# The first expert block of a mixture-of-experts stage written ahead of its loop and of the block table, with 16-bit operands in the router

## What is computed

```python
logits = (h @ w_router).astype(jnp.float32) + b_router      # h: [512, 1024], 32 experts
topv, idx = lax.top_k(logits, TOP_K)                        # 4
gates = jax.nn.softmax(topv, axis=-1)
...
gu = xblk @ w_gate_up[e] + b_gate_up[e]                     # [1024, 2048] for each expert
gate = jnp.minimum(gu[:, :D_FF], SWIGLU_LIMIT)
up = jnp.clip(gu[:, D_FF:], -SWIGLU_LIMIT, SWIGLU_LIMIT)
act = (up + 1.0) * (gate * jax.nn.sigmoid(SWIGLU_ALPHA * gate))
return act @ w_down[e] + b_down[e]                          # [1024, 1024] for each expert
```

## Time and profile before

| | |
|---|---|
| median of 3 runs | 2981.27 us (2976.05 to 2981.37) |
| the profiled execution | 2982.14 us |
| its span in the trace | 2980.3 us |
| PE busy | 2805.3 us, 94% |
| DVE busy | 1319.7 us, 44% |
| ACT busy | 829.6 us, 28% |
| DMA in the span | 587.90 MB, mean 197 GB/s |
| weight chunks of the experts | 192 of 2048 KB, median 24.1 us from issue to landing |

### The profile page before, as it was taken

How to read it: one execution, slowest core, us unless ns; L and a number is a source line. 1 busy time by engine, 2 the same in 40 slices (tenths; PEclk the granted TensorE clock), 3 DMA queues, 4 the chain that set the end, 5 groups by cost and what they waited for, 6 DMA issues and landing times.

```text
span 2980.3 us, 44597 instructions
## 1 busy us (share of the span) xinstructions
PE 2805.3 (94%) x16220; PEld 1781.0 (60%) x16221; DVE 1319.7 (44%) x2773; ACT 829.6 (28%) x1663; POOL 103.1 (3%) x118
## 2 busy tenths in 40 slices
PE   9999999988999989998999899999999999999999
PEld 7888668743333333333333387585787695666884
DVE  6774686442232222222222455535564454444662
ACT  3321662212222222222222223414121224323211
POOL 0000000000000000000000000011000000110000
PEclk9999999978999999999999999999999999999999
DMA  3224312257999999999999831031321321112212
GB/s 143 85 71 138 120 52 85 76 209 317 416 423 415 414 410 410 414 413 407 412 413 413 337 117 69 29 110 36 106 85 57 105 101 43 68 64 78 85 57 85
DMA packets 115239, 587.90 MB, mean 197 GB/s; under 512 B 12714, under 2 KB 18218, under 8 KB 89507
## 3 DMA queue, kind: packets, MB, share of 16 engines
q1 hardware_dynamic: 105890, 569.26, 48.4%
q0 software_dynamic: 9216, 16.90, 1.5%
HBM read 572.91 MB, written 29.88 MB: 202 GB/s over the span
## 4 chain that ended last, share of the span: by engine, by line
PE 80%; DMA 12%; DVE 5%; issue 2%; ACT 2%; DVEq 1%; ACTq 0%; SPq 0%; POOLq 0%
PE banks L422 37%; DMA arena<-in_w_experts 11%; PE banks L1757 11%; PE banks L355 5%; PE banks L1799 5%; PE banks L989 4%; PE banks L916 3%; PE banks L1765 2%; PE banks L1805 2%; PE banks L1004 2%; PE banks L978 2%; PE banks L294 1%; PE banks L1243 1%; PE banks L952 1%; PE banks L1736 1%
## 5 line engine op out<-in xcount | busy, mean ns | idle before, releaser
L422 PE MATMUL banks<-arena 128*128 128x256 f32 (+2 forms) x5376 | 1156.1, 376 | 12.7 <-ACT arena L459 6.0
L422 PEld LDWEIGHTS banks<-arena 128*128 128x128 f32 x5376 | 1005.4, 190 | 147.8 <-issue 14.1
L1757 PE MATMUL banks<-arena 128*64 128x512 f32 x2048 | 466.7, 601 | 48.4 <-DMA arena<-in_w_experts 34.2
L1757 PEld LDWEIGHTS banks<-arena 128*64 128x64 f32 x2048 | 156.2, 137 | 315.2 <-issue 313.0
L459 ACT ACTIVATE arena<-banks 128x512 f32<-128x512 f32 (+2 forms) x220 | 129.9, 590 | 699.5 <-PE banks L422 696.6
L407 DVE TENSOR_TENSOR arena<-arena 128x1024 f32<-128x1024 f32 (+2 forms) x220 | 235.8, 1072 | 50.6 <-issue 26.4
L1938 DVE TENSOR_TENSOR arena<-banks,arena 128x512 f32<-128x512 f32 x64 | 44.3, 692 | 462.7 <-PE banks L1783 236.5
L1799 PE MATMUL banks<-arena 128*64 128x512 f32 x1024 | 237.8, 600 | 1.6 <-DMA arena<-in_w_experts 1.1
L475 DVE TENSOR_TENSOR arena<-banks,arena 128x512 f32<-128x512 f32 (+2 forms) x123 | 83.5, 680 | 273.6 <-PE banks L422 269.8
L355 PE MATMUL banks<-arena 128*128 128x512 f32 x384 | 166.8, 592 | 0.0
L1799 PEld LDWEIGHTS banks<-arena 128*64 128x64 f32 x1024 | 67.6, 135 | 129.1 <-issue 129.1
(11 more groups left out here) (269 smaller groups left out, 2388.3 us busy)
## 6 DMA issues: line engine op xcount, KB each, us to landing
arena<-in_w_experts SPq DMA_DIRECT2D x192, 2048.0 KB, 24.1
arena<-in_w_in SPq DMA_DIRECT2D x76, 1024.0 KB, 4.9
arena<-in_w_out SPq DMA_DIRECT2D x12, 1024.0 KB, 5.0
arena<-in_w_branch SPq DMA_DIRECT2D x24, 512.0 KB, 4.6
expert_rows<-arena SPq DMA_DIRECT2D x1, 8192.0 KB, 30.2
arena<-expert_rows SPq DMA_DIRECT2D x4, 2048.0 KB, 18.0
arena<-in_w_in SPq DMA_DIRECT2D x2, 2048.0 KB, 9.1
arena<-in_w_in SPq DMA_DIRECT2D x4, 832.0 KB, 4.9
```

What stands on the lines that cost most here:

```text
L422: last = PE.matmul(PS[:, bank, t * width:(t + 1) * width], one[:, t * P:(t + 1) * P], other, start=(first and t == 0 and kk == 0), stop=(t ...
L1757: last = PE.matmul(PS[HB * s:HB * (s + 1), 4 + h], xT[:, k, 0:HB], gate_up(2 * h + s, k), start=(k == 0), stop=(k == 7))
```

## The change

Router and experts are woven into each other. In the router, `oh`, the slot values (`slot_of`), the rows and the places they are compared with (`row_h`, `places_h`) become float16; the rows are scaled to whole numbers first. The gate matrix is built later, behind the keys. DVE's lists are made in two calls: the first block's alone, then (after `cnt`, `nb`, `cum`, block 0's `FEW` and `LAST`, and a new semaphore `first_rdy`) the other 191. PE, ACT and POOL start the expert stage at `first_rdy`. PE runs block 0 as code of its own, ahead of the loop, and between its products it does what the router's `pe_` did: ranking, keys, turning the gates, placing the table. SP still needs the table; it stores the gate matrix (`GATES_T`) and reads the last expert's row back in 96 copies, which takes the place of PE's product (line 1743). DVE makes the last block's selection in that block. The cut diff:

```diff
+        def rank_kinds(pe):
+            pe.wait_ge(SEM["kinds_rdy"], up(1))
+            PE.matmul(PS[:, 1, 200:202], v(CO["before"], P), v(KINDS, 2), start=True, stop=True)
+            PE.matmul(PS[:, 1, 202:204], v(CO["ones"], P), v(KINDS, 2), start=True, stop=True).then_inc(SEM["ranked"], 1)
+        def spread_keys(pe):
+            pe.wait_ge(SEM["keys_rdy"], up(1))
+            PE.matmul(PS[:, 1, 256:384], v(CO["ones"], P), v(KEYS, P), start=True, stop=True).then_inc(SEM["keys_mm"], 1)
+        def rows_of_table(pe):
+            pe.wait_ge(SEM["column_rdy"], up(1))
+            for q, col in enumerate((FOUND, FOUND + 4, FOUND + 5)):
+                last = PE.matmul(PS[0:1, 1, 64 * q:64 * q + 64], v(col, 1), v(PLACES, 64), start=True, stop=True)
+            last.then_inc(SEM["row_mm"], 1)
+        def turn_gates(pe):
+            pe.wait_ge(SEM["gmat_rdy"], up(1))
+            for tt in range(TT):
+                gates = v(R + 1536 + NE * tt, NE)
+                PE.transpose(PS[0:NE, 6, tt * P:(tt + 1) * P], gates, ident)
+                last = PE.matmul(PS[BS:P, 7, tt * P:(tt + 1) * P], gates, ident, start=True, stop=True, tile_position=(0, BS))
+            last.then_inc(SEM["gt_mm"], 1)
...
             lg, mx, ix, e4, idxf = (v2(R, TT, NE), v2(R + 128, TT, 8), v2(R + 160, TT, 8),
                                     v2(R + 192, TT, 4), v2(R + 208, TT, 4))
-            oh = v2(R + 256, 16, NE)
+            oh = v(R + 256, 8 * NE).bitcast(F16).rearrange("p (a e) -> p a e", a=16)
+            slot_of = v(R + 1856, 8 * LPE).bitcast(F16).rearrange("p (b a) -> p b a", b=LPE)
+            row_h, places_h = v(R + 768, 8).bitcast(F16), v(R + 784, P // 2).bitcast(F16)
...
             def dve_(dve, c):
...
                 V.memset(v(NOM, NE), 0.0)
-                oh4 = v3(R + 256, TT, 4, NE)
+                V.memset(v(BE, 1, 1), 0.0)
+                V.memset(v(BCOL, 1, 1), 0.0)
+                oh4 = oh.rearrange("p (t k) e -> p t k e", t=TT)
+                V.tensor_scalar(places_h, v(CO["iota_p"], P), 1.0 / PART, None, ALU.mult)
...
                     V.tensor_tensor(lg[:, tt], PS[:, tt, 0:NE], brow, ALU.add)
...
-                V.tensor_tensor(tmp, oh, v(GATES, 16).unsqueeze(2).to_broadcast([P, 16, NE]), ALU.mult)
-                V.drain()
-                V.tensor_reduce(Gm, v3(R + 896, TT, 4, NE).rearrange("p t k e -> p t e k"), AX.X, ALU.add)
-                V.drain().then_inc(SEM["gmat_rdy"], 1)
...
@@ -1556,14 +1568,16 @@
                 V.tensor_copy(blk_f, at_b)
                 V.drain()
                 V.scalar_tensor_tensor(row_f, blk_f, -float(BS * PART), addrf, ALU.mult, ALU.add)
+                V.drain()
+                V.tensor_scalar(row_h, row_f, 1.0 / PART, None, ALU.mult)
                 for b in range(LPE):
-                    V.scalar_tensor_tensor(v(R + 1856 + 16 * b, 16), blk_f, float(b), v(CO["slot1"], 16), ALU.is_equal, ALU.mult)
+                    V.scalar_tensor_tensor(slot_of[:, b], blk_f, float(b), v(CO["slot1"], 16), ALU.is_equal, ALU.mult)
                 V.drain()
                 for b in range(LPE):
-                    V.tensor_tensor(slots[:, :, b], oh, v(R + 1856 + 16 * b, 16).unsqueeze(2).to_broadcast([P, 16, NE]), ALU.mult)
+                    V.tensor_tensor(slots[:, :, b], oh, slot_of[:, b].unsqueeze(2).to_broadcast([P, 16, NE]), ALU.mult)
                 for tt in range(TT):
-                    V.tensor_tensor(rows_at[:, 4 * tt:4 * tt + 4], v(CO["iota_p"], P).unsqueeze(1).to_broadcast([P, 4, P]),
-                                    row_f[:, 4 * tt:4 * tt + 4].unsqueeze(2).to_broadcast([P, 4, P]), ALU.is_equal)
+                    V.tensor_tensor(rows_at[:, 4 * tt:4 * tt + 4], places_h.unsqueeze(1).to_broadcast([P, 4, P]),
+                                    row_h[:, 4 * tt:4 * tt + 4].unsqueeze(2).to_broadcast([P, 4, P]), ALU.is_equal)
                     V.drain().then_inc(SEM["addr_rdy"], 1)
...
+                def rows_of_lists(first, n):
+                    nobody, found_, rows_, tokens = (v(o + first, n) for o in (R + 1856, TAB + 1024, ALLR, ALLT))
+                    V.tensor_scalar(nobody, PS[:, 0, first:first + n], 0.0, float(1 << 20), ALU.is_equal, ALU.mult)
+                    V.drain()
+                    V.scalar_tensor_tensor(found_, PS[:, 0, first:first + n], -1.0, nobody, ALU.add, ALU.add)
+                    V.drain()
+                    V.tensor_copy(rows_.bitcast(I32), found_)
+                    V.drain()
+                    V.tensor_scalar(tokens.bitcast(I32), rows_.bitcast(I32), 2, None, ALU.logical_shift_right)
+                    V.drain()
+                dve.wait_ge(SEM["listed"], up(1))
+                rows_of_lists(0, 1)
+                V.tensor_copy(v(TOK, 1).bitcast(I32), v(ALLT, 1).bitcast(I32)).then_inc(SEM["tok_rdy"], 1)
                 V.tensor_copy(cnt, PS[:, 1, 128:160])
...
-                nobody = v(R + 256, LISTS)
-                dve.wait_ge(SEM["listed"], up(1))
-                V.tensor_scalar(nobody, PS[:, 0, 0:LISTS], 0.0, float(1 << 20), ALU.is_equal, ALU.mult)
-                V.drain()
-                V.scalar_tensor_tensor(v(R + 512, LISTS), PS[:, 0, 0:LISTS], -1.0, nobody, ALU.add, ALU.add)
-                V.drain()
-                V.tensor_copy(v(ALLR, LISTS).bitcast(I32), v(R + 512, LISTS))
-                V.drain()
-                V.tensor_scalar(v(ALLT, LISTS).bitcast(I32), v(ALLR, LISTS).bitcast(I32), 2, None, ALU.logical_shift_right)
-                V.drain()
-                V.tensor_copy(v(TOK, 1).bitcast(I32), v(ALLT, 1).bitcast(I32)).then_inc(SEM["tok_rdy"], 1)
+                V.tensor_scalar(v(FEW, 1, 1).bitcast(I32), cnt[0:1, 0:1], float(P // 2), None, ALU.is_le)
+                V.tensor_scalar(v(LAST, 1, 1).bitcast(I32), cum[0:1, NE - 1:NE], -1.0, None, ALU.add)
+                V.drain().then_inc(SEM["first_rdy"], 1)
+                rows_of_lists(1, LISTS - 1)
...
                 V.drain().then_inc(SEM["keys_rdy"], 1)
+                V.tensor_tensor(tmp, oh, v(GATES, 16).unsqueeze(2).to_broadcast([P, 16, NE]), ALU.mult)
+                V.drain()
+                V.tensor_reduce(Gm, v3(R + 896, TT, 4, NE).rearrange("p t k e -> p t e k"), AX.X, ALU.add)
+                V.drain().then_inc(SEM["gmat_rdy"], 1)
...
                 V.drain().then_inc(SEM["column_rdy"], 1)
                 dve.wait_ge(SEM["row_mm"], up(1))
-                V.tensor_copy(v(BE, 192, 1).bitcast(I32), PS[0:1, 1, 0:192])
-                V.tensor_scalar(v(LAST, 1, 1).bitcast(I32), cum[0:1, NE - 1:NE], -1.0, None, ALU.add)
+                V.tensor_copy(v2(BE, 3, 64, 1).bitcast(I32)[:, :, 1:64], PS[0:1, 1, 0:192].rearrange("p (a b) -> p a b", a=3)[:, :, 1:64])
                 V.drain().then_inc(SEM["table_rdy"], 1)
...
             def sp_(sp, c):
+                sp.wait_ge(SEM["gt_rdy"], up(1))
+                sp.dma_start(GATES_T, v(GT, S, NE)).then_inc(SEM["gates_out"], 16)
                 sp.wait_ge(SEM["table_rdy"], up(1))
                 norm_pre.lead(sp, c)
                 final = last_block(sp)
+                e_last = entry(sp, BE, final, NE - 1)
+                sp.wait_ge(SEM["gates_out"], 16)
+                sp.dma_start(v(SEL, S, BS), GATES_T[bass.ds(e_last, 1)].rearrange("o t -> (o t)").partition_broadcast(BS)).then_inc(SEM["share_in"], 16)
                 with sp.Fori(1, final + 1) as j:
...
             def pe_(pe, c):
-                pe.wait_ge(SEM["table_rdy"], up(1))
+                pe.wait_ge(SEM["first_rdy"], up(1))
...
                     last.then_inc(SEM["xt"], 1)
                 gather_T(1)
-                pe.wait_ge(SEM["one_rdy"], up(1))
-                pe.wait_ge(SEM["gt_rdy"], up(1))
-                PE.matmul(PS[:, 7], v(ONE_E, P, NE), v(GT, S, NE), start=True, stop=True).then_inc(SEM["share_mm"], 1)
-                with pe.Fori(0, final + 1) as j:
+                rank_kinds(pe)
+                def block(j):
+                    first = isinstance(j, int)
...
                         apart(pe, j)
-                        pe.wait_ge(SEM["sel_made"], up(1))
...
@@ -1814,20 +1841,35 @@
                                 arrived(2 * h + kh)
                                 if h and kh:
                                     turn_products(0, more)
-                                last = products(h, ks)
+                                if first and h + kh == 0:
+                                    products(h, ks[:2])
+                                    spread_keys(pe)
+                                    turn_gates(pe)
+                                    last = products(h, ks[2:])
+                                    rows_of_table(pe)
+                                else:
+                                    last = products(h, ks)
                                 if more:
                                     last = more_products(h, ks)
                                 last.then_inc(SEM["ch_free"], 2)
```

(39 more changed lines are left out.)

31 lines of the change are left out of this document (4 added, 27 removed).

## The result

The changed kernel takes **2990.36 us** (median of 5 runs, 2987.32 to 2992.62) where the kernel before, run beside it, takes 2981.27 (5 runs, 2976.05 to 2983.32): a ratio of **1.0036, with an interval of 1.0023 to 1.0049**. The forecast was 2979.0 with a range up to 2984.5. The change makes the kernel slower, and the range did not hold it. The profiled execution after took 2987.32 (span 2985.5).

What follows compares the result with a forecast made beforehand. DMA was taken to bound the expert loop (0.99, 413 GB/s), timed from its first weight issue. 3.2 - 0.8 = 2.4 us off the profiled 2982.14 gave 2979.7; with the median 0.9 lower, the forecast was 2979, range 2972 to 2984.5.

Steps and rivals of the forecast that it cites:

- The bound of the loop: Expert loop: DMA-bound at 0.99 and 413 GB/s for 973 us, ending a fixed time after its first weight issue.
- rival 3: Expert loop: the head start fills the DMA queue better, 5 us on top, giving 2974; chance 0.21.
- Gate matrix, counts, token numbers: Router on DVE: net gain of 0.35 us before the list products; token numbers at 665.9 instead of 667.9.
- The ten passes: Router on DVE: 16-bit inputs to ten 512-element passes save nothing, at most 3.3 us.
- The first gather: Ahead of PE's transposes: issued at 666.85, landing 4.6 us later at 671.45.
- the 0.8 us set down for block 1's gather: Start of the expert loop: this gather now runs beside the first weights, costing 0.8 us, bounds 0 and 1.2.
- The table: Block table at the router's end: ready at 684.1, 6.6 us later than before.
- SP's piece: Table to first weight issue on SP: 3.3 us, issue at 687.4, 3.2 us earlier; bounds 2.5 to 5.
- rival 4: SP's first weight issue gets no earlier, with the table at 685.9; 2981 to 2983 us, chance 0.15.
- It may hold block 0 by some 3 us; PE began the block 9 us earlier and hides that: DVE's wait for block 1's gather ahead of block 0's activations: some 3 us, hidden by PE's 9 us lead.
- Rival 5: Passage from single block 0 to loop: PE's stand could come twice, 6.9 us more, giving 2988; chance 0.07.
- The sum: Whole kernel: 3.2 gained less 0.8 given back, 2.4 us off the expert loop, nothing changed after it.

Runs made afterwards that it cites:

- g1: e2 with the long branch of PE's single block 0 placed ahead of its short one; 2983.68 us, ratio 1.0009.
- g2: g1 with the branches swapped inside PE's loop too, long one first; 2987.61 us, ratio 1.0022.
- g3: g1 with SP issuing block 1's six chunks before the gains and the last expert's gates; 2984.20 us, ratio 1.0008.
- e2: The changed kernel with DVE's wait for the next block's gather moved from ahead of a block's activations to behind their first half; 2985.48 us, ratio 1.0021.
- h3: e2 with sixteen semaphore increments added to PE's router stream, moving its later code 16 instructions further; 2981.76 us, ratio 1.0006.
- e1: The kernel before with only PE's block 0 taken out of its loop and written ahead of it; 2983.89 us, ratio 1.0011.
- f1: The kernel before plus 128 empty PE instructions that the compiled program lacks, so a plain repeat; 2980.27 us, ratio 1.0009.
- h2: e2 with five semaphore increments added to PE's router stream, moving its later code five instructions further; 2985.32 us, ratio 1.0014.

## Why the prediction was wrong, point by point

**The bound of the loop, half right.** "The expert loop ends a fixed time after its first weight chunk is issued" failed. Over the fourteen executions whose first issue lies at A + 24.2 to 26.1 (all but g1, g2 and g3), the first combine load follows PE's start of block 2, from 74.2 to 86.7, with a slope of 1.04 by least squares, and none is off by more than 2.1 us. With the first issue at 24.87 the repeat of the changed kernel ends its loop no earlier. In g1, where PE is early and the issue 4.6 us late, the other end shows: 1019.8, with PE waiting for weights. So both have to be on time; g3, whose issue is nearly on time and whose loop is still 4.2 us late, says that this is not all. The evidence was read and filed under rival 3 only as a chance to gain: in the loop's first 280 us the chain has no weight transfer in it, so PE sets the pace there, and what it loses the queues lose. For a change of PE's stream that is the first term of the sum and not a rival.

**Gate matrix, counts, token numbers: right.** The gather was issued at 665.19, at A + 1.94; before at A + 4.20. That is 2.3 us earlier; the forecast was 2.0.

**The ten passes: right**: 3.70 and 3.12 with 16-bit operands, 3.71 and 3.12 without. "Vector Engine (DVE) Microarchitecture Reference" in the Trainium skill (5.1) measured one element read 16 times as an input of such a pass at the single rate, and the trace agrees for 32 and 128 times; of the doubled rate of the tier table nothing shows in these passes. That the repeated element is the reason is not shown, since no run has such a pass without one.

**The first gather: mis-sized.** The forecast took the 4.6 us of the earlier trace rows. That row is the middle of two, 5.0 and 4.1. Issued beside the transfer of chunk 0, it held PE's transposes for longer, to 672.25:

```profile
665.19 1.23 POOL L1450 DMA_INDIRECT arena<-h_rows,arena  x1 [16.99 <-DVE arena L1602]
...
687.97 1.00 POOL L1450 DMA_INDIRECT arena<-h_rows,arena  x1 [20.58 <-DVE arena L1948]
```

The rows landed at A + 9.0 where the forecast had 671.45 - 664.66 = A + 6.8: 2.2 us late, and no more than 0.2 earlier than before (668.86 + 5.0 = A + 9.2). That the chunk's transfer is the cause is argued, not shown. The 0.5 MB taken for a gather are also too much: the queue of gathers and scatters moved 16.90 MB in the whole span before, half of what 33 and 31 of that size come to. It changes only the 0.8 us set down for block 1's gather.

**The table: the working right, its start late.** It was forecast ready at 684.1, A + 19.4, and is at 684.85 + 0.34, A + 21.9. Of these 2.5 us 2.2 are the gather's; from there to the table, router visits and all, it is 12.9 us, forecast 12.65:

```profile
684.85 0.34 DVE L1680 CAST arena<-banks 1x189 int32<-1x189 f32 x1 [3.90 <-PE banks L1469]
```

**SP's piece: mis-sized.** From the table (685.19) to the first issue (689.24) are 4.05 us, forecast 3.3 and inside its bounds of 2.5 to 5. Together 2.5 + 0.75 = 3.25 us, all of the 3.2 that the first issue was to gain. In its effect this is rival 4, which had 0.15.

**"It may hold block 0 by some 3 us; PE began the block 9 us earlier and hides that": the step that failed.** The wait for block 1's gather was seen and costed at nothing. It is 9.19 us for DVE and 5.79 for PE. The lead is no 9 us where it is needed: from A the first products come 7.1 us earlier, the last ones ahead of the wait (695.83 against 701.23 before) only 4.0, because the router visits stand between them. The wait takes 5.79 where there was one of 0.88, and behind it PE is 0.9 us late. e2 removes it and gives 4.9 us of the median back, about half of the loss.

**Rival 5 was the other half of the mechanism, at 0.07.** It said that a seam and the back edge could cost PE's stand twice. They do: 6.32 + 4.42 against 4.38, 6.4 us more in stands alone, where the rival had 6.9 with the low clock behind them. That it came so near is in part luck, since the seam's price hangs on the place of the code (3.86 to 10.89 in e2's variants). The rival's condition, "only if PE's lead (some 5 us) is used up and fewer chunks are in flight than the queues need", held, and both halves could have been read: the chain of before has PE and no transfer in just these microseconds. Its 2988 was 2.4 short; it did not have the wait for the gather.

**The sum as it came out.** Nothing gained at the first issue. PE against the kernel before, from A: 4.0 us early ahead of the wait, 0.9 late behind it (701.62 against 702.12), 2.4 late at the end of block 0 (711.66 against 710.62; the granted clock from 701 to 712 us is 0.82, before 1.00), 8.7 late at block 2. Of these last 6.3 us the stands are 6.4. The combine loads start 8.7 later, the span ends 6.6 later from A, and the median is 9.1 up.

## What to carry to other kernels

A chain of waits without a transfer in it says who sets the pace in that stretch, whatever the mean share of the queues is; price a change of that engine there first, at full. When a wait is moved ahead of a block, compare what waits for it with the lead at the end of the block, not with the lead at its start. Taking one pass out of a loop with branches changes which code the engine jumps over, and the price of a jump (0 to 11 us here) hangs on where the code happens to lie: look for idle time without a releaser behind the first blocks, and compare versions only after moving the code by a few instructions.

## What had not been expected of the hardware

- Sixteen semaphore increments in a place where PE waits anyway took 4.0 us off a stand and 3.7 us off a kernel's median (e2 to h3; their intervals, 1.0012 to 1.0029 and 0.9996 to 1.0016, just overlap), and five added 3.1 us to that stand (7.84 to 10.89) without a change of the median. That is as large as what the change was about.
- A stand costs the same 4 us beside idle DMA queues (4.24 in g1, at a DMA share of 0.02; 4.21 and 4.46 at the same place in g2 and g3) as beside full ones (4.14 to 4.57 behind block 0 in e1, the kernel before and f1).
- The clock falls around a stand. The stretch with the seam, for h2 and then for the kernel before (columns as above, PE's granted clock ahead of the DMA share):

```profile
700.00:730.00 30.00, 18.87 (x82) 6.35 (x80) 1.90 (x5) 3.44 (x5) 1.01 (x1) 0.77 0.95 387
```

```profile
700.00:730.00 30.00, 24.74 (x118) 8.87 (x116) 6.76 (x15) 6.25 (x10) 2.00 (x2) 0.89 1.00 418
```

With a stand of 10.89 us in it the clock stands at 0.77 on average, before at 0.89 with one of 4.38. Behind either stand the first 48 records take 12.96 and 13.11 us, in g1, where block 1 has no stand ahead of it, 10.52: some 2.5 us of what a stand costs come behind it, in products at the low of the two levels.
